# High and low parts of the activations in one 512-column pass over the high weights

## What is computed

```python
def swiglu(h, w_gate, w_up, w_down):
    return (jax.nn.silu(h @ w_gate) * (h @ w_up)) @ w_down
...
    for l in range(DEPTH):            # first block
        h = rms_norm(x, pre_mix_g[l])
        mix = parallel_mixer(...)     # h @ w_in, RG-LRU, forgetting attention, retention, @ w_out
        x = x + rms_norm(mix, post_mix_g[l])
        h = rms_norm(x, pre_cross_g[l])
        x = x + rms_norm(memory_cross_attention(...), post_cross_g[l])
        h = rms_norm(x, pre_ffn_g[l])
        x = x + rms_norm(swiglu(h, w_gate[l], w_up[l], w_down[l]), post_ffn_g[l])
...
    for l in range(DEPTH):            # second block
        x = x + 0.5 * swiglu_2(rms_norm_2(x, ffn1_norm[l]), ...)
        ... = jnp.split(rms_norm_2(x, mix_norm[l]) @ w_in[l], ...)   # three kinds of attention, gated
        x = x + merged @ w_out[l]
        x = x + 0.5 * swiglu_2(rms_norm_2(x, ffn2_norm[l]), ...)
```

## Time and profile before

| | |
|---|---|
| Time, median of 3 runs | 2451.25 us (2448.5 to 2456.89) |
| Profiled execution | 2452.91 us, its span 2451.1 us |
| TensorE matmuls | 2206.5 us busy, 90%, 17158 instructions |
| VectorE | 1425.4 us busy, 58% |
| ScalarE | 1135.3 us busy, 46% |
| Mean granted TensorE clock | 0.954 of full speed |
| Weights moved | 664 DMAs of 512 KB, HBM read 354.25 MB |

### The profile page before, as it was taken

One profiled execution on the slowest core, in us unless ns is written; L12 is line 12 of the kernel. 1 busy time (PEld: TensorE's weight loads), 2 busy tenths in 40 slices (PEclk: granted clock), 3 DMA queues, 4 the chain that ended last, 5 costly groups with the idle time before them and its releaser, 6 DMA issues.

```text
span 2451.1 us, 40437 instructions
## 1 busy us (share of the span) xinstructions
PE 2206.5 (90%) x17158; PEld 2112.1 (86%) x17158; DVE 1425.4 (58%) x2194; ACT 1135.3 (46%) x1745; POOL 81.0 (3%) x81
## 2 busy tenths in 40 slices
PE   2888879997978889979998998899999998988999
PEld 2877779997867889979997887899999988878998
DVE  3454656546546465565557455755655574657664
ACT  3354444443544444444445446544444444465442
POOL 4000000000000000010000000000000000000000
PEclk9888899998988999989999899999999998999999
DMA  5632425563423345645554223455556552234554
GB/s 130 188 108 75 149 75 179 182 206 121 138 69 121 125 138 181 199 146 188 184 190 160 71 86 104 160 189 190 173 189 193 170 165 92 87 102 139 182 180 155
DMA packets 97956, 360.28 MB, mean 147 GB/s; under 512 B 11064, under 2 KB 11065, under 8 KB 97264
## 3 DMA queue, kind: packets, MB, share of 16 engines
q1 hardware_dynamic: 95616, 348.17, 43.6%
q0 software_dynamic: 1728, 6.38, 1.4%
q10 hardware_dynamic: 432, 3.15, 0.3%
HBM read 354.25 MB, written 3.41 MB: 146 GB/s over the span
## 4 chain that ended last, share of the span: by engine, by line
PE 73%; DVE 14%; ACT 8%; issue 3%; DMA 2%; POOL 1%; ACTq 0%; DVEq 0%; POOLq 0%
PE bank L270 65%; DVE w_lo L1261 3%; ACT w_hi L782 2%; PE bank L322 1%; DMA raw<-in_stream 1%; DVE xn_lo L1283 1%; PE bank L642 1%; DVE sq L1318 1%; PE bank L306 1%; POOL sq L1869 1%; PE bank L327 1%; DVE x L1322 1%; DVE sq L1825 1%; PE bank L323 1%; PE bank L615 1%
## 5 line engine op out<-in xcount | busy, mean ns | idle before, releaser
L1261 DVE TENSOR_TENSOR w_lo<-raw,w_hi 128x1024 fp32r<-128x1024 f32 x664 | 803.1, 1245 | 429.7 <-ACT w_hi L782 429.6
L270 PE MATMUL bank<-xn_hi,w_hi 128*128 128x256 f32 x3168 | 914.0, 289 | 114.1 <-DVE xn_lo L1283 90.8
L270 PE MATMUL bank<-xn_lo,w_hi 128*128 128x256 f32 x3168 | 906.0, 286 | 0.0
L270 PE MATMUL bank<-xn_hi,w_lo 128*128 128x256 f32 x3168 | 905.3, 286 | 0.0
L782 ACT ACTIVATE w_hi<-raw 128x1024 fp32r<-128x1024 f32 x664 | 672.2, 1049 | 265.5 <-PE bank L270 246.7
L270 PEld LDWEIGHTS bank<-xn_hi,w_hi 128*128 128x128 f32 x3168 | 618.1, 195 | 128.2 <-issue 114.2
L270 PEld LDWEIGHTS bank<-xn_lo,w_hi 128*128 128x128 f32 x3168 | 618.3, 195 | 0.2
L270 PEld LDWEIGHTS bank<-xn_hi,w_lo 128*128 128x128 f32 x3168 | 617.8, 195 | 0.0
L270 PE MATMUL bank<-hid_hi,w_hi 128*128 128x256 f32 x1056 | 291.5, 276 | 0.0
L270 PE MATMUL bank<-hid_lo,w_hi 128*128 128x256 f32 x1056 | 291.5, 276 | 0.0
L270 PE MATMUL bank<-hid_hi,w_lo 128*128 128x256 f32 x1056 | 291.5, 276 | 0.0
(11 more groups left out here) (344 smaller groups left out, 2758.5 us busy)
## 6 DMA issues: line engine op xcount, KB each, us to landing
raw<-in_stream SPq DMA_DIRECT2D x664, 512.0 KB, 4.2
skew<-logit POOLq DMA_DIRECT2D x1, 2304.0 KB, 35.6
table<-skew POOLq DMA_DIRECT2D x1, 1408.0 KB, 7.3
logit<-in_small POOLq DMA_DIRECT2D x4, 288.5 KB, 3.2
con<-in_con ACTq DMA_DIRECT2D x1, 1029.0 KB, 7.0
xn<-in_mem ACTq DMA_DIRECT2D x1, 1024.0 KB, 11.5
x<-in_x ACTq DMA_DIRECT2D x1, 1024.0 KB, 15.0
out<-x POOLq DMA_DIRECT2D x1, 1024.0 KB, 4.2
```

The source lines that it names most:

```text
L270: m = T.matmul(out, a, b, start=first and j == 0, stop=True, skip_group_check=True)
L1261: V.tensor_tensor(w_lo[m % RING], raw[m % RING], w_hi[m % RING].bitcast(F32), ALU.subtract).then_inc(*lo_done.next())
```

## The change

High and low part of an activation tile now lie side by side in one buffer of 2 x 256 columns (`xs`, `y`, `hid`, `mem`, `merged_in`), and so do those of the weights (`w`). A new `slot_wide` makes two passes per weight tile (`wide_products`): the high weights over all 512 columns, into two halves of a bank, and the low weights over the 256 high columns, into the first half. A slot's result is then two banks, a `quad`; `quad[0]` and `quad[1]` alternate for gate, up and projections, `quad[1]` and `quad[2]` for wo, co and down of block 1 and down of block 2. The halves are added when read: ScalarE copies the second half to SBUF (`copy_low`), VectorE adds the first half to it (`add_high`), and the steps on the result then work from SBUF. TensorE waits for that sum (`gate_summed`, `up_summed`, `proj_summed`, `out_made`) before it takes the quad again. wo of block 2 is added to `x` in two steps straight from the banks. The slots of `slot_rows`, of the memory's keys, of the branch gates and up-projections of block 2, and f, sk, wkv and the compression keep their three passes. In a feed-forward the two halves of `ahead` now stand apart on ScalarE and VectorE.

```diff
-    hid_hi = sb_at("hid_hi", [P, FT, S], F32R, base)
-    hid_lo = sb_at("hid_lo", [P, FT, S], F32R, base + FT * 1024)
+
+    hid = sb_at("hid", [P, FT, 2, S], F32R, base)
...
-    w_hi = [sb(f"w_hi{r}", [P, HK, COLS], F32R) for r in range(RING)]
-    w_lo = [sb(f"w_lo{r}", [P, HK, COLS], F32R) for r in range(RING)]
+    w = [sb(f"w{r}", [P, HK, 2, COLS], F32R) for r in range(RING)]
...
-    xn_hi, xn_lo = sb("xn_hi", [P, KT, S], F32R), sb("xn_lo", [P, KT, S], F32R)
-    y_hi, y_lo = sb("y_hi", [P, KT, S], F32R), sb("y_lo", [P, KT, S], F32R)
+    xs = sb("xs", [P, KT, 2, S], F32R)
+    y = sb("y", [P, KT, 2, S], F32R)
...
+    quad = [banks[:, 2 * i:2 * i + 2, :].rearrange("p c (a s) -> p c a s", a=2) for i in range(4)]
...
+    out_n = xn
...
+        def wide_products(out, one, both, first):
+
+            T.matmul(out, one[0], both, start=first, stop=True, skip_group_check=True)
+            return T.matmul(out[:, 0, :], one[1], both[:, 0, :], start=False, stop=True, skip_group_check=True)
...
+                for ct in range(2):
                     for k in range(HK):
-                        m = products(out[:, ct, :], tile(r, k, slice(ct * P, (ct + 1) * P)),
-                                     [t[:, half * HK + k, :] for t in (hi, lo)], half == 0 and k == 0 and ct == cts[0])
+                        m = wide_products(out[:, ct, :, :], tile(r, k, slice(ct * P, (ct + 1) * P)),
+                                          act[:, half * HK + k, :, :], half == 0 and k == 0)
                 m.then_inc(*half_used.next())
...
             for j in range(FB):
                 if j:
-                    T.wait_ge(*up_read.at(FB * f + j))
-                slot_T((f, "up", j), dense[1], xn_hi, xn_lo)
+                    T.wait_ge(*up_summed.at(FB * f + j))
+                slot_wide((f, "up", j), quad[1], xs)
                 if j + 1 < FB:
-                    T.wait_ge(*gate_read.at(FB * f + j + 1))
-                    slot_T((f, "gate", j + 1), dense[0], xn_hi, xn_lo)
+                    T.wait_ge(*gate_summed.at(FB * f + j + 1))
+                    slot_wide((f, "gate", j + 1), quad[0], xs)
...
+                        if b >= 2 and k == 0:
+                            T.wait_ge(*out_made.at(out_no(f, b - 2)))
                         for ct in range(2):
-                            m = products(acc[b][:, ct, :], tile(r, part, slice(ct * P, (ct + 1) * P)),
-                                         [t[:, k, :] for t in (hid_hi, hid_lo)], k == ct == 0)
+                            m = wide_products(quad[(2, 1)[b % 2]][:, ct, :, :], tile(r, part, slice(ct * P, (ct + 1) * P)),
+                                              hid[:, k, :, :], k == 0)
...
+        def copy_low(dst, q, done):
+
+            AC.activation(dst, q[:, :, 1, :], ACT.Copy).then_inc(*done.next())
...
             norm_in(i, gain, pairs)
             ahead((f, "gate", 0))
             norm_scale(n)
-            silu(0)
             for j in range(FB):
-                ahead((f, "up", j))
-                hidden(j)
+                AC.wait_ge(*slot_end((f, "gate", j)))
+                if j:
+                    AC.wait_ge(*hid_made.at(FB * f + j))
+                copy_low(act_t, quad[0], gate_copied)
+                ahead((f, "up", j), (0,))
+                AC.wait_ge(*gate_scaled.at(FB * f + j + 1))
+                AC.activation(act_t, act_t, ACT.Silu).then_inc(*silu_made.next())
+                ahead((f, "up", j), (1,))
+                AC.wait_ge(*slot_end((f, "up", j)))
+                copy_low(rinv, quad[1], up_copied)
                 if j + 1 < FB:
-                    ahead((f, "gate", j + 1))
-                    silu(j + 1)
+                    ahead((f, "gate", j + 1), (0,))
+                AC.wait_ge(*hid_full.at(FB * f + j + 1))
+                AC.activation(hid_hi[:, 2 * j:2 * j + 2, :], act_t, ACT.Copy).then_inc(*hid_hi_made.next())
+                if j + 1 < FB:
+                    ahead((f, "gate", j + 1), (1,))
...
+            def out_low(name, b, q):
+                AC.wait_ge(*slot_end(name))
+                copy_low(out_n[:, pair_of(b), :], q, out_copied)
+
             for b in range(4):
                 ahead(at(f"wo{b}"))
-            norm_add(norm_no(L, 0, True), {b: slot_end(at(f"wo{b}")) for b in range(4)})
+                if b:
+                    out_low(at(f"wo{b - 1}"), b - 1, quad[1 + (b - 1) % 2])
+            out_low(at("wo3"), 3, quad[2])
+            norm_add(norm_no(L, 0, True), {b: out_made.at(12 * L + b + 1) for b in range(4)})
...
+            squares_of(3)
+            norm_add(norm_no(L, 2, True), {3: out_made.at(out_no(L, 3))}, L + 1)
...
+        def add_high(dst, q, copied, done):
+
+            V.wait_ge(*copied.at(done.n + 1))
+            V.tensor_tensor(dst, q[:, :, 0, :], dst, ALU.add).then_inc(*done.next())
+            V.wait_ge(*done.last())
...
             def silu(j):
-                V.wait_ge(*slot_end((f, "gate", j)))
-                if j:
-                    V.wait_ge(*hid_made.at(FB * f + j))
-                V.tensor_tensor(act_t, dense[0], scale_2, ALU.mult).then_inc(*gate_read.next())
+                add_high(act_t, quad[0], gate_copied, gate_summed)
+                V.tensor_tensor(act_t, act_t, scale_2, ALU.mult).then_inc(*gate_scaled.next())
 
             def hidden(j):
-                V.wait_ge(*slot_end((f, "up", j)))
+                add_high(rinv, quad[1], up_copied, up_summed)
                 V.wait_ge(*silu_made.at(FB * f + j + 1))
-                V.tensor_tensor(act_t, act_t, dense[1], ALU.mult).then_inc(*up_read.next())
-                V.wait_ge(*up_read.last())
+                V.tensor_tensor(act_t, act_t, rinv, ALU.mult).then_inc(*hid_full.next())
+                if j + 1 < FB:
+                    ahead((f, "gate", j + 1), (0,))
+                V.wait_ge(*hid_full.last())
                 low_half(hid_lo[:, 2 * j:2 * j + 2, :], act_t, hid_hi[:, 2 * j:2 * j + 2, :],
                          hid_hi_made.at(FB * f + j + 1), hid_made)
...
+                sum_out(quad[(2, 1)[b % 2]], b)
+                V.scalar_tensor_tensor(sq[:, pair_of(b), :], out_n[:, pair_of(b), :], 0.5, scale_2, ALU.mult, ALU.mult
+                                       ).then_inc(*own.next())
...
+                high, low = (quad[(0, 1, 2, 1)[b]][:, :, half, :] for half in range(2))
+                V.tensor_tensor(x[:, pair_of(b), :], x[:, pair_of(b), :], high, ALU.add).then_inc(*own.next())
+                V.wait_ge(*own.last())
+                V.tensor_tensor(x[:, pair_of(b), :], x[:, pair_of(b), :], low, ALU.add).then_inc(*x_updated.next())
```

247 lines of the change are left out of this document (156 added, 91 removed).

## The result

The changed kernel is slower: 2485.22 us (2476.28 to 2486.15) against 2449.88 us beside it, ratio 1.0132 (1.010 to 1.0165). A second measurement, in experiment 4, gave 1.0128 (1.0112 to 1.0144). The forecast was 2406. The profiled execution took 2476.28 us, 2474.4 of it span.

The account below looks back on a forecast made before the run. TensorE was taken as the bound, its 256-column passes too short to hide a weight load. 2451.1 us less 79 gained there plus 34 for uncovered steps gave 2406, range 2395 to 2420 (chance 0.60), wider range 2378 to 2440.

Parts of the forecast that it names:

- the second paragraph on the bound: TensorE's steady stream: a weight load takes some 110 ns, so a 256-column pass is too short by 6 to 13 ns.
- rival 1: Load sticking out shrinks to 113.4 ns for xs and y too, as buffers change place: 97 us gained, 2388 us; chance 0.12.
- The size of the 512-column pass: On TensorE, the pass of high weights over 512 columns takes 216 ns, like the f32 pass of equal length.
- My own sign of being wrong: The forecast is wrong if the 512 pass takes 225 ns or more, or if TensorE idles between slots.
- the gain of 79 us: TensorE's wide slots: gate and up 49.3, down 11.3, mixers 17.3, wo of block 2 1.2; bounds 45 and 115 us.
- The dear ends of the tile: Each pass keeps its present extra: a tile takes 346.7 or 333.3 ns and gains 13.3 or 6.7 ns.
- rival 3: Extra belongs to columns, not load: 512 pass 240 ns, tile 360 as before, only 34 us stay, 2485 us; chance 0.04.
- The steps at the ends: Stage ends where nothing hides the new copies and adds from TensorE: 34 us together, between 25 and 42.
- each wo and co end: Block 1, four places: copy, table load, dummy root and four squares follow TensorE's end; 3.9 us later, 15.6 in all.
- three ends of block 2's feed-forwards: Block 2's feed-forwards, four places: copy and add come ahead of the half update; 1.45 us each, 5.8 in all.
- the two wo of block 2: Two places in block 2: two adds in place of one, 0.7 us each, 1.4 in all.
- rival 4: VectorE becomes the bound in gate and up slots, the 49 us there are lost, 2455 us; chance 0.06.

Follow-up runs that it names:

- experiment 4: Matmul streams alone, in bursts of 32 equal tiles each behind a pass of another width; and the unaltered changed kernel run again: 2483.76 us, ratio 1.0128.
- experiment 1: The changed kernel with each 512-column pass cut into two of 256 columns, all copies, adds and waits kept: 2496.90 us, ratio 1.0185.

## Why the prediction was wrong

**The step that failed is the second paragraph on the bound.** It said "a 128x128 weight load takes some 110 ns", so "A 256-column pass is thus just too short to hide a load, by 6 to 13 ns". The 0.11 us between passes of 128 columns is real (112 ns alone as well). But it did not give the extra of longer passes: with 32-column weights a 512-column pass is not shorter by more than 2 ns, and with the same loads the 120 and 113.4 ns both turn into 118 when only an address moves. Whether a load of some 112 ns has a part in the 113.4 stays open, since no run had 256 columns with smaller weights. Two rows spoke against me and I read past them: the same instruction, load included, took 120 ns with xn and 113.4 with hid. By its size alone a load can't stick out by two amounts. My rival 1 saw that difference and left its cause open.

**The size of the 512-column pass** was taken from plain f32, a pass of equal length and another kind: 216 ns there, 227 to 237 for split operands. My own sign of being wrong, 225 ns or more, was there: 232 to 237 ns in gate, up and down of the changed kernel. So a tile fell not to 336 and 329.4 ns but to 346.7 or 353.4, and the gain of 79 us came down to some 12: gate and up 19 instead of 49, down -14 instead of +11, the rest in the mixers. The dear ends of the tile, 346.7 ns with xn and 333.3 with hid, left out most of what arrived: 353.4 for gate and up in four of six feed-forwards, and for down in all. That a 512 pass could cost as much as the two it replaces was in rival 3 alone. That it could cost more, as in down (235 ns against 2 x 113.4), was in none.

**Rival 3** named the time, 2485, and the sign of the evidence (a 512 pass above 229 ns). It got 0.04, on the strength of rows 4 and 5, which say nothing about columns of split operands. Its mechanism, something that lasts as long as the two operands are read, is nearer to what the runs show than mine, but not shown: the extra is not in proportion to the columns (7 to 13 ns at 256, 13 to 23 at 512), and its price (tile 360, steps 34) met the measured total by luck, with two terms that were both off (tile 347 to 353, steps 45).

**The steps at the ends**, 34 us with an upper end of 42, were 45. Places and order were right, three sizes were not. Against the kernel before, slot starts in the kernel of experiment 1 come later by 5.2 us at each wo and co end (said 3.9: the mean square starts 4.2 later and takes 0.95 longer, at the lower clock); by 2.8 us at three ends of block 2's feed-forwards (said 1.45: nq0's wait grows from 0.88 to 2.2 us and its second half then runs at 0.56 of the clock); by 3.6 and 1.3 us behind the two wo of block 2 (said 0.7). Those behind cq3 (1.35, said 1.45), nc and sq (2.1 to 2.4, said 2.2) and block 1's feed-forwards (2.25, said 2.0) held. I had priced each wait by its own length, and left out that a longer one slows what stands behind it.

**What held:** VectorE and ScalarE stay hidden in gate and up (rival 4 is out), splits keep 1243 ns in the new layout, copy and add 597 and 692 ns, and TensorE doesn't idle between the slots of gate, up and down.

## What to carry to other kernels

Where two streams of equal instructions run at different paces, find the difference between them (here the operands' addresses) before naming a cause that is the same in both; streams of matmuls alone, at several widths and addresses, show what the pace goes with. The price of a new operand form is taken from a row with the same data type and both operands, and if there is none, its range reaches at least to the sum of the parts that it replaces. A step put between TensorE's last pass and the next one costs its length and, where the wait grows long enough for the clock to fall as here, the time that what follows takes longer.

## What the hardware showed that was not expected

- At full clock a stream of split operands (three 256-column passes, or 512 and 256) falls to one of a few paces, 340, 346.7, 353.4 or 360 ns a tile (values between them for some distances), and keeps it for a stage. At half the clock the extra is gone: in nq0 of the changed kernel, behind its wait, passes start 0.42 and 0.21 us apart, which is their columns at 1.2 GHz:

```profile
1287.12 0.63 PE L288 MATMUL banks<-xs,w 128*128 128x512 f32 x1
...
1287.54 0.42 PE L289 MATMUL banks<-xs,w 128*128 128x256 f32 x1
1287.75 0.63 PE L288 MATMUL banks<-xs,w 128*128 128x512 f32 x1
```

- The paces go with the distance between weights and moving operand modulo 256 bytes. At 64 or 192 three passes can have 340 ns, at 0 they have 360; for a pair 32 or 160 are best, 346.7. Why is not known. 192 unused bytes were worth 0.9% of this kernel.
- A pass of plain f32 at 512 columns takes 429 ns, two clocks a column, and one of bf16 216, one clock a column, both within 3 ns, on operands whose addresses were not varied.
